# Norm factors by logarithm and exponential on ScalarE, and the last tile scaled in pairs of chunks

## The reference

```
def rmsnorm(x, g):
    y = x * lax.rsqrt(jnp.mean(x * x, axis=-1, keepdims=True) + EPS)
    return y * g

h = rmsnorm(x, g_mix);  z = h @ w_in
a_out = sliding-window attention with sinks      # 512 wide
b_out = gated linear recurrence * gelu(gate)     # 256 wide
c_out = short gated convolution                  # 256 wide
merged = concat([rmsnorm(a_out), rmsnorm(b_out), rmsnorm(c_out)])   # each with its part of g_out
x = x + merged @ w_out
up = rmsnorm(x, g_ffn) @ w_up
u, gt = split(causal_conv3(up))
x = x + (silu(gt) * u) @ w_down
y = rmsnorm(x, g_final)
```

## Time and profile before

| | us |
|---|---|
| median of 3 runs | 1124.78 (1124.31 to 1125.24) |
| the profiled execution | 1124.28 |
| its span, first to last instruction | 1122.5 |
| PE busy | 1099.5 |
| DVE busy | 795.8 |
| ACT busy | 332.8 |
| POOL busy | 18.8 |

### The profile page before, as it was taken

The page is one execution under the profiler, slowest core; times in us unless marked ns, Lnnn a source line. Parts: engine busy times, 40 slices in busy tenths (PEclk is TensorE's granted clock), DMA queues, the critical chain, the costliest instruction groups (busy, mean ns, idle before and its releaser), DMA issues.

```text
span 1122.5 us, 18120 instructions
## 1 busy us (share of the span) xinstructions
PE 1099.5 (98%) x6996; PEld 1069.2 (95%) x6996; DVE 795.8 (71%) x1524; ACT 332.8 (30%) x538; POOL 18.8 (2%) x30
## 2 busy tenths in 40 slices
PE   7999999999999999999999999999999999999995
PEld 6999988888999999999999999999999999999994
DVE  6963788998977866757666667565666667576778
ACT  7443445576456211111111111111111111111243
POOL 0000000000000000000000000000000000000004
PEclk9999999999999999999999999999999999999998
DMA  6311210125442111111111111111111111111104
GB/s 250 103 38 34 94 39 20 38 77 201 140 147 79 39 57 39 40 54 47 47 37 56 50 44 37 56 37 56 37 56 37 56 37 42 52 53 42 38 16 151
DMA packets 25178, 72.17 MB, mean 64 GB/s; under 512 B 3472, under 2 KB 10000, under 8 KB 25104
## 3 DMA queue, kind: packets, MB, share of 16 engines
q1 hardware_dynamic: 24992, 71.45, 18.5%
q10 hardware_dynamic: 144, 0.15, 0.1%
HBM read 66.76 MB, written 5.87 MB: 65 GB/s over the span
## 4 chain that ended last, share of the span: by engine, by line
PE 90%; DVE 6%; ACT 1%; issue 1%; DMA 1%; SPq 0%; DVEq 0%; ACTq 0%
PE psum L1538 70%; PE psum L1745 7%; PE psum L1575 2%; PE psum L1604 2%; PE psum L1606 2%; PE psum L1605 2%; PE psum L1691 1%; PE psum L1641 1%; PE psum L1681 1%; DMA x_sb<-in_x 1%; PE psum L1629 1%; PE psum L1591 1%; DVE zb L1432 0%; DVE att L1443 0%; DVE zb L975 0%
## 5 line engine op out<-in xcount | busy, mean ns | idle before, releaser
L1538 PE MATMUL psum<-h_hi,w_hi 128*128 128x344 f32 x1176 | 379.2, 322 | 0.5 <-DVE zb L1308 0.5
L1538 PE MATMUL psum<-h_lo,w_hi 128*128 128x344 f32 x1176 | 376.2, 320 | 0.0
L1538 PE MATMUL psum<-h_hi,w_lo 128*128 128x344 f32 x1176 | 376.1, 320 | 0.0
L550 ACT ACTIVATE w_hi<-raw 128x1024 fp32r<-128x1024 f32 x88 | 93.1, 1058 | 447.6 <-PE psum L1538 424.2
L1538 PEld LDWEIGHTS psum<-h_hi,w_hi 128*128 128x128 f32 x1176 | 221.2, 188 | 1.9 <-issue 0.8
L1538 PEld LDWEIGHTS psum<-h_lo,w_hi 128*128 128x128 f32 x1176 | 221.1, 188 | 0.9
L1538 PEld LDWEIGHTS psum<-h_hi,w_lo 128*128 128x128 f32 x1176 | 221.4, 188 | 0.0
L1349 DVE TENSOR_TENSOR x_sb<-psum,x_sb 128x344 f32<-128x344 f32 x240 | 121.6, 515 | 79.6 <-PE psum L1538 79.5
L1538 PE MATMUL psum<-act_hi,w_hi 128*128 128x344 f32 x480 | 153.9, 321 | 1.0 <-DVE x_sb L1349 1.0
L1538 PE MATMUL psum<-act_hi,w_lo 128*128 128x344 f32 x480 | 154.5, 322 | 0.0
L1538 PE MATMUL psum<-act_lo,w_hi 128*128 128x344 f32 x480 | 153.7, 320 | 0.0
(11 more groups left out here) (240 smaller groups left out, 1560.7 us busy)
## 6 DMA issues: line engine op xcount, KB each, us to landing
raw<-in_w SPq DMA_DIRECT2D x106, 512.0 KB, 3.2
x_sb<-in_x SPq DMA_DIRECT2D x8, 516.0 KB, 4.9
out_y<-x_sb SPq DMA_DIRECT2D x12, 344.0 KB, 2.5
x_sb<-in_x SPq DMA_DIRECT2D x2, 1376.0 KB, 11.4
x_sb<-in_x SPq DMA_DIRECT2D x4, 344.0 KB, 5.4
zb<-in_ck SPq DMA_DIRECT2D x1, 512.0 KB, 3.6
zb<-in_cv SPq DMA_DIRECT2D x1, 512.0 KB, 4.5
out_k_old<-in_k_keep SPq DMA_DIRECT2D x1, 508.0 KB, 5.8
```

Source lines behind the costliest of these rows:

```text
L550: nc.scalar.activation(split_hi[split_of(s)][:, :], raw[s % RAW][:, :], ACT.Copy).then_inc(w_hi_ready, 1)
L1538: ins = mm(out, a, b, start=(at == 0), stop=(at == n - 1))
```

## The change

All 18 factors are now made on ACT alone: the logarithm of the mean of squares plus eps, and then the exponential of minus one half of it, in place. ACT waits for its own logarithm, and signals the factor by `rstd_ready` (at the end `fin_rstd_ready`). DVE has no reciprocal left there and only waits for the factor, at the same places in its list. PE's wait before it writes the sum of the next tile at the end is for the logarithm instead of the root. At the end ACT multiplies all 24 chunks by the gain, and DVE scales two chunks by one multiplication with the factor, five launches in all. The two small launches that load the root's table early now load the logarithm's.

```diff
-            def root(name, dst, width):
+            def factor(name, dst, width):
                 act.wait_ge(task_done, done_at(name))
-                nc.scalar.activation(dst, (side_ps if name in SIDE else task_ps)[:, 0:TW], ACT.Sqrt, bias=eps[:, 0:1],
+                nc.scalar.activation(dst, (side_ps if name in SIDE else task_ps)[:, 0:TW], ACT.Ln, bias=eps[:, 0:1],
                                      scale=1.0 / width).then_inc(read_a, 1)
+                act.wait_ge(read_a, read_at(name))
+                nc.scalar.activation(dst, dst, ACT.Exp, scale=-0.5).then_inc(rstd_ready, 1)
...
-            def reciprocal(name, dst):
-                dve.wait_ge(read_a, read_at(name))
-                link(V.reciprocal(dst, dst))
+            def factor_wait(name):
+                dve.wait_ge(rstd_ready, read_at(name))
...
-            def fin_root(t):
+            def fin_factor(t):
                 act.wait_ge(fin_sum_done, sum(u <= t for u, _ in FIN_GROUPS))
-                nc.scalar.activation(rstd[:, tile(t)], task_ps[:, 0:TW], ACT.Sqrt, bias=eps[:, 0:1],
-                                     scale=1.0 / D).then_inc(fin_root_done, 1)
+                nc.scalar.activation(rstd[:, tile(t)], task_ps[:, 0:TW], ACT.Ln, bias=eps[:, 0:1],
+                                     scale=1.0 / D).then_inc(fin_log_done, 1)
+                act.wait_ge(fin_log_done, t + 1)
+                nc.scalar.activation(rstd[:, tile(t)], rstd[:, tile(t)], ACT.Exp, scale=-0.5).then_inc(fin_rstd_ready, 1)
...
                     fin_square(t, m)
                     if t and m == 2:
-                        fin_root(t - 1)
-                    if t < NT - 2 or t == NT - 2 and m < FIN_POOL:
-                        fin_gain(t, m)
-            fin_root(NT - 1)
+                        fin_factor(t - 1)
+                    fin_gain(t, m)
+            fin_factor(NT - 1)
...
-                ins = V.scalar_tensor_tensor(out=x_sb[:, m, tile(t)], in0=x_sb[:, m, tile(t)], scalar=gain_fin[:, m:m + 1],
-                                             in1=rstd[:, tile(t)], op0=ALU.mult, op1=ALU.mult)
-                if m % 2:
-                    ins.then_inc(y_last_ready, 1)
+                dve.wait_ge(fin_gain_done, KD * t + m + 2)
+                V.tensor_tensor(x_sb[:, m:m + 2, tile(t)], x_sb[:, m:m + 2, tile(t)],
+                                rstd[:, tile(t)].unsqueeze(1).broadcast_to([P, 2, TW]), ALU.mult).then_inc(y_last_ready, 1)
...
-                    if t and m == 4:
-                        fin_reciprocal(t - 1)
             dve.wait_ge(fin_rstd_ready, NT - 1)
-            for m in range(FIN_POOL, KD):
+            for m in range(FIN_POOL, KD, 2):
                 fin_scale(NT - 2, m)
-            fin_reciprocal(NT - 1)
             dve.wait_ge(fin_rstd_ready, NT)
-            for m in range(KD):
+            for m in range(0, KD, 2):
                 fin_scale(NT - 1, m)
```

More of the change, by code:

```diff
@@ L582, in _ @@
                     hi(2)
-            root(("norm", "x", 0), rstd[:, tile(0)], D)
+            factor(("norm", "x", 0), rstd[:, tile(0)], D)
             for t in range(1, NT):
@@ L586, in _ @@
             hi(3)
-            root(("norm", "x", 1), rstd[:, tile(1)], D)
-            root(("norm", "x", 2), rstd[:, tile(2)], D)
+            factor(("norm", "x", 1), rstd[:, tile(1)], D)
+            factor(("norm", "x", 2), rstd[:, tile(2)], D)
             act.wait_ge(lam_ready, 1)
@@ L635, in _ @@
             for t in range(NT):
-                root(("norm", "B", t), rstd_b[:, tile(t)], 2 * P)
+                factor(("norm", "B", t), rstd_b[:, tile(t)], 2 * P)
             def exps(u):
@@ L704, in _ @@
                     act.wait_ge(kv_stored, 16 * 2)
-                    root(("norm", "A", 0), rstd_a[0], HG * P)
+                    factor(("norm", "A", 0), rstd_a[0], HG * P)
                 if i == 13:
@@ L709, in _ @@
                 if i == 14:
-                    root(("norm", "C", 0), rstd_c[0], 2 * P)
+                    factor(("norm", "C", 0), rstd_c[0], 2 * P)
                 if i == 15:
@@ L725, in _ @@
             hi(OUT_SLOT0 + 2)
-            root(("norm", "A", 1), rstd_a[1], HG * P)
+            factor(("norm", "A", 1), rstd_a[1], HG * P)
             probs_t_copy(UNITS - 1)
@@ L751, in _ @@
                 if o == 18:
-                    root(("norm", "X", 0), rstd[:, tile(0)], D)
-            root(("norm", "X", 1), rstd[:, tile(1)], D)
+                    factor(("norm", "X", 0), rstd[:, tile(0)], D)
+            factor(("norm", "X", 1), rstd[:, tile(1)], D)
             x2_hi(2, 0, KD)
-            root(("norm", "X", 2), rstd[:, tile(2)], D)
+            factor(("norm", "X", 2), rstd[:, tile(2)], D)
             def silu(n, i=None):
@@ L909, in _ @@
             x_split(2, range(KD))
-            reciprocal(("norm", "x", 0), rstd[:, tile(0)])
+            factor_wait(("norm", "x", 0))
             evac(0, k_sb)
@@ L917, in _ @@
             evac(1, x_pad[:, 3:])
-            reciprocal(("norm", "x", 1), rstd[:, tile(1)])
+            factor_wait(("norm", "x", 1))
             evac(2, k_sb)
             evac(3, x_pad[:, 3:])
-            reciprocal(("norm", "x", 2), rstd[:, tile(2)])
+            factor_wait(("norm", "x", 2))
             evac(4, k_sb)
@@ L1092, in _ @@
                 if 28 <= j < 30:
-                    reciprocal(("norm", "B", j - 28), rstd_b[:, tile(j - 28)])
+                    factor_wait(("norm", "B", j - 28))
                 if s in LX_SLOTS:
@@ L1217, in _ @@
                 if i == 0:
-                    reciprocal(("norm", "B", NT - 1), rstd_b[:, tile(NT - 1)])
+                    factor_wait(("norm", "B", NT - 1))
                 if i == 2:
@@ L1227, in _ @@
                 if i == 10:
-                    reciprocal(("norm", "A", 0), rstd_a[0])
+                    factor_wait(("norm", "A", 0))
                     a_scale(0)
@@ L1266, in _ @@
                 if o == 0:
-                    reciprocal(("norm", "A", 1), rstd_a[1])
+                    factor_wait(("norm", "A", 1))
                     w_lo_ffn(OUT_SLOT0 + 3)
@@ L1277, in _ @@
                 if o == 4:
-                    reciprocal(("norm", "C", 1), rstd_c[1])
+                    factor_wait(("norm", "C", 1))
                     c_scale(1)
@@ L1282, in _ @@
                 if o == 7:
-                    reciprocal(("norm", "A", 2), rstd_a[2])
+                    factor_wait(("norm", "A", 2))
                 if o == 8:
@@ L1286, in _ @@
                 if o == 9:
-                    reciprocal(("norm", "C", 2), rstd_c[2])
+                    factor_wait(("norm", "C", 2))
                 if o == 10:
@@ L1296, in _ @@
                 if o == 20:
-                    reciprocal(("norm", "X", 0), rstd[:, tile(0)])
+                    factor_wait(("norm", "X", 0))
             V.memset(pad_g[:, 0:2], 0.0)
@@ L1352, in _ @@
             w_lo_ffn(FFN_SLOT0 + 2)
-            reciprocal(("norm", "X", 1), rstd[:, tile(1)])
+            factor_wait(("norm", "X", 1))
             carry_in(0, pad_g)
@@ L1358, in _ @@
                 if f == 4:
-                    reciprocal(("norm", "X", 2), rstd[:, tile(2)])
+                    factor_wait(("norm", "X", 2))
                 ffn_evac(FFN_JOB0 + f, t, (pad_g, pad_u)[s], None, first_ps[f])
```

21 lines of the change are left out of this document (9 added, 12 removed).

## The result

| | before | changed |
|---|---|---|
| median of ten runs | 1124.72 us (1124.31 to 1125.53) | 1128.33 us (1127.63 to 1129.04) |
| profiled execution, its span | 1124.28, 1122.5 us | 1129.02, 1127.3 us |

The ratio is 1.0031, 95% interval 1.0024 to 1.0039: slower, as predicted, by 3.6 us where 3.1 were predicted, and inside the range. The ten times of the changed kernel stand in two groups of five, 1127.63 to 1128.08 and 1128.58 to 1129.04, and the median lies between them; experiments 9 to 11 say what parts them. In the later comparisons the kernel before had a median of 1124.35 (21 executions; experiments 1, 2, 3 and 8) and of 1124.41 (27; experiments 4 to 7), and against these the change cost 3.9 to 4.0 us.

The account below looks back on a forecast made before the run. PE was taken to bound the kernel, so ACT and DVE work counts only where PE waits or after its last product. Start 0.6, projection 0.9, end 1.5: 1124.78 + 3.1 = 1127.9 us, range 1125.2 to 1130.3.

Parts of the forecast that it names:

- start: First 35 us: DVE waits for a square put back by ACT's load, and PE loses 0.6 us (0.5 to 0.9).
- attention: Factors A0 and C0: no wait of PE there that DVE's queue ends, so nothing was counted.
- output projection: Boundary of tiles 0 and 1: later weight splits delay c_lo(1), and PE waits 0.9 us (0 to 1.5).
- FFN entry, X0 to X2: These factors delay w_lo parts by up to 3 us, mostly within slack (X2's sum has 1 us); counted 0.
- scaling starts, at full clock: End: ACT's queue of squares, gains and loads lets DVE scale at 1117.65 instead of 1115.46, 2.2 us later.
- lower clock of the last product: End: PE idles some 2.5 us before its last job and may then run at 1.2 GHz, costing up to 0.3.
- first scaling to the end: End: four scalings on 688 columns in 3.2 us, last landing about 6.1 us after the first starts.
- sum: Whole kernel: start 0.6, output projection 0.9 and end 1.5 give +3.0 to 3.1 us.
- The cost of a factor: Each factor adds 1.86 us to ACT's queue, or 3.15 if the logarithm's own load isn't hidden in a wait.
- rival (A): Output projection hides its delay; only start and end count: +2.1, 1126.9 us; chance 0.20.
- rival (B): Later w_hi splits pass on to weight loads and FFN entry: another 1 to 2 us, 1129.5; chance 0.20.
- Rival (C): All factors: logarithm and exponential come from one loaded table, so none switches: 4.7 us less, 1120.1; chance 0.05.

Follow-up runs that it names:

- experiments 9 to 11: Unedited repeats: the changed kernel twice (1127.48 and 1128.50 us), the kernel before with only the end changed once (1125.95 us).
- experiments 1, 2, 3 and 8: Kernel before with changed end, 1126.81 us; changed kernel with old end, 1125.93; with one table set, 1119.88; with end sums one product later, 1128.54.
- experiments 4 to 7: Changed kernel, one table set for the end, 1122.18 us; one set everywhere, eight scalings, 1120.05; kernel before plus pairs, 1125.33; changed, factor behind split, 1127.44.
- Experiment 7: Changed kernel with factor A of tile 2 in the output projection set behind ACT's next weight split: 1127.44 us, ratio to before 1.0024.
- experiment 1: Kernel before with only the end changed (three factors by logarithm and exponential, all gains on ACT, pair scaling): 1126.81 us, ratio 1.0019.
- experiment 6: Kernel before with all gains of the end on ACT and pair scaling, roots and reciprocals kept: 1125.33 us, ratio 1.0004.
- experiment 2: Changed kernel with the end of the kernel before, so only the 15 other factors are changed: 1125.93 us, ratio 1.0013.

## Why the prediction was right, and what was mis-sized

| term | predicted | measured |
|---|---|---|
| start | 0.6 | 0.62, also with the 15 factors alone (time from ahead of the first factor taken off) |
| attention | 0 | 0.0 (offset of PE 0.87 to 0.90 from 36 to 200 us) |
| output projection | 0.9 | 0.97 to 1.02 at PE's wait for c_lo (six traces), and up to 0.25 ahead of it |
| FFN entry, X0 to X2 | 0 | 0.0 |
| scaling starts, at full clock | 2.2 | 2.14 to 2.17 |
| lower clock of the last product | 0.2 taken, up to 0.3 | 0 or 1.0 |
| first scaling to the end | -0.9 | -0.35 |
| sum | 3.1 | 3.6 at full clock, 4.5 at the lower one (three traces of the changed kernel); medians 3.6 to 4.0 |

- **The cost of a factor** was right: load 1.28, logarithm 0.55, exponential 0.49 and 0.40 to the next launch. The estimate of the exponential from a square of that shape gave 0.48. The 2.66 us that the Trainium skill ("ScalarE: Activation LUTs", What ACT_TABLE_LOAD costs) gives for a switch, drain included, isn't what stood here: the exponential starts 1.29 to 1.30 us after its load does.
- **The start** was right in mechanism and size. The tree was predicted at 30.45 and started at 30.66, 0.25 of which came from ahead of the change.
- **The projection** was right step by step: split 292.10 (predicted 291.2, with 0.88 of offset), DVE's w_lo 2.65 later, c_lo 2.65 later. PE's loss at this wait is 1.0 and not 0.9, of which 0.73 is the wait itself. Experiment 7 shows the cause by taking it away; rival (A) falls by it, and rival (B) by the constant offset behind it.
- **The end** was right up to the scaling: experiment 1 has both times to within 0.05 us, and PE's idle time of 2.31 to 2.34 us was predicted as 2.5. Two sizes were off. The first is a subtraction. The prediction had the last landing at 1123.8 and took from it 1122.5, which is the end of the span before. The landing itself was right. In the changed kernel's trace the last issue of L478 (window 1123.5 to 1127.3 us) and its time to landing are

```profile
L478 SPq DMA_DIRECT2D out_y<-x_sb x1: 373/373/373, 1123.9 to 1123.9; - x1
DMA to landing us min/median/max: 3.0/3.0/3.0
```

so it lands at 1126.8, 6.2 after the scaling starts (predicted 6.1), and the span goes on for 0.45 behind it. Before, the last transfer is issued at 1119.5 and lands 2.6 later, at 1122.0, and the same 0.45 follows. Those 0.45 were left out, so the pairs gave 0.35 us and not 0.9; pairs and gains alone (experiment 6) have the same 6.7. The second is the lower clock, "up to 0.3"; it costs 1.0 where it comes, since the six matmuls take 1.94 us instead of 1.05 and the sums ahead of them are slowed too. At full clock the output's 0.55 and the projection's 0.1 to 0.3, less the 0.2 taken for the clock, make the 0.5 us between 3.1 and 3.6; at the lower clock another 1.0 comes on top. That the medians differ by no more than 3.6 owes something to luck, as half the executions got the full clock and the ten of before came out 0.3 to 0.4 above the later ones.
- **Rival (C)** was priced well (1120.1 against 1119.88) and was no outcome of this kernel only because the program as listed switched: 46 loads. The change would have been a gain of 0.4% with three more lines. The Trainium skill's rule on table sets and the listing pointed to different outcomes, and the listing decided. That the price came within 0.2 is in part luck: the start gained 0.66 instead of 0.3, while the scaling started 0.3 later than its 1111.8 (1111.23 with an offset of -0.85; the logarithm waits 0.80 for PE's sum) and the output took the same 0.5 longer as above.

## What to carry to other kernels

Count the table loads in the listing before anything else is priced: one set holds logarithm and exponential, but a load stood before each of them until that set was loaded by hand, and that turned +0.3% into -0.4%. On an engine that runs at 34%, 1.3 us still counts where a weight split stands behind it in the queue, so look at what is queued behind an added instruction, not at its engine's load. A stretch limited by output transfers is hardly shortened by faster arithmetic ahead of it: halving the launches of the last tile brought 0.2 to 0.35 us, less than the 0.7 that the gains moved to ACT for it cost in experiment 6. And when a predicted end is compared with a measured one, both must be the same event: the last landing and the end of the span are 0.45 us apart here.

## What the runs showed of the hardware

- A table load is 1.28 us in every trace here, whether a root, a logarithm or an exponential follows; 1.29 to 1.30 from its start to that of the next launch.
- With PE idle 2.31 to 2.34 us ahead of it, the last product ran at a granted clock of 1.00 in three executions and of 0.50 in three; 1.0 us hangs on it, a quarter of the whole difference measured. After 2.08 and 2.09 us of idle PE its last four sums took 1.43 us in one execution (before) and 2.66 in another (experiment 2).
- Four transfers of 352 KB behind one another, from the first issue to the end of the span, took 5.8 us (1121.52 to 1127.3), at 360 GB/s while the engines were full (1124 to 1126 us); the last landing is 0.45 us before the end.
